# Wide moving operand for the gate and up units of the second block

## The reference

```python
def swiglu_2(x, w_gate, w_up, w_down):
    return (jax.nn.silu(x @ w_gate) * (x @ w_up)) @ w_down

def rmsnorm_2(x, g):
    x32 = x.astype(jnp.float32)
    y = x32 * lax.rsqrt(jnp.mean(x32 * x32, axis=-1, keepdims=True) + EPS)
    return (y * g.astype(jnp.float32)).astype(x.dtype)

# hybrid_layer, called for two layers
x = x + 0.5 * swiglu_2(rmsnorm_2(x, ffn1_norm), ffn1_gate, ffn1_up, ffn1_down)
...                                    # the mixers
x = x + 0.5 * swiglu_2(rmsnorm_2(x, ffn2_norm), ffn2_gate, ffn2_up, ffn2_down)
```

## Time and profile before

| | us |
|---|---|
| median of three runs | 2867.47 |
| span of the profiled execution | 2866.6 |
| TensorE busy | 2796.4 (98%) |
| VectorE busy | 1820.9 (64%) |
| ScalarE busy | 1341.1 (47%) |
| GpSimd busy | 789.2 (28%) |

### The profile page before, as it was taken

How to read it: one execution, slowest core, us unless ns; L and a number is a source line. 1 busy time by engine, 2 the same in 40 slices (tenths; PEclk the granted TensorE clock), 3 DMA queues, 4 the chain that set the end, 5 groups by cost and what they waited for, 6 DMA issues and landing times.

```text
span 2866.6 us, 59491 instructions
## 1 busy us (share of the span) xinstructions
PE 2796.4 (98%) x23696; PEld 2684.6 (94%) x23696; DVE 1820.9 (64%) x2505; ACT 1341.1 (47%) x1872; POOL 789.2 (28%) x768
## 2 busy tenths in 40 slices
PE   6999999999999999999999999999999999999999
PEld 4999999999999999999987898999889999997999
DVE  4655746687647557566466765665876566488664
ACT  3434434444435444344345444445764444377443
POOL 1322411123304214133001330320743223146330
PEclk9999999999999999999999999999999999999999
DMA  8765666575666756766631454555325555541554
GB/s 304 256 243 205 231 232 209 193 248 193 235 233 204 243 202 209 240 201 230 239 104 60 147 183 154 176 193 184 131 82 186 195 174 184 192 156 60 178 183 152
DMA packets 151712, 546.44 MB, mean 191 GB/s; under 512 B 16688, under 2 KB 20576, under 8 KB 151136
## 3 DMA queue, kind: packets, MB, share of 16 engines
q1 hardware_dynamic: 147632, 534.84, 54.9%
q10 hardware_dynamic: 3888, 8.86, 0.9%
HBM read 541.80 MB, written 1.84 MB: 190 GB/s over the span
## 4 chain that ended last, share of the span: by engine, by line
PE 91%; DVE 5%; ACT 1%; issue 1%; ACTq 1%; DMA 0%; SPq 0%; DVEq 0%
PE ps L410 28%; PE ps L412 28%; PE ps L411 28%; PE ps L437 2%; DVE w_lo L390 1%; PE ps L821 1%; PE ps L805 1%; PE ps L794 1%; ACTq L1558 0%; DVE xT L1952 0%; DVE h_lo L1602 0%; DVE xT L1968 0%; PE ps L889 0%; PE ps L696 0%; DVE m L1967 0%
## 5 line engine op out<-in xcount | busy, mean ns | idle before, releaser
L390 DVE TENSOR_TENSOR w_lo<-raw,w_hi 128x1024 fp32r<-128x1024 f32 x874 | 1135.4, 1315 | 634.5 <-ACT w_hi L382 632.1
L410 PE MATMUL ps<-h_hi,w_hi 128*128 128x256 f32 (+1 forms) x4928 | 1405.8, 285 | 24.3 <-DVE h_lo L1602 12.2
L412 PE MATMUL ps<-h_hi,w_lo 128*128 128x256 f32 (+1 forms) x4928 | 1393.8, 283 | 0.0
L411 PE MATMUL ps<-h_lo,w_hi 128*128 128x256 f32 (+1 forms) x4928 | 1388.5, 282 | 0.0
L382 ACT ACTIVATE w_hi<-raw 128x1024 fp32r<-128x1024 f32 x874 | 894.4, 1053 | 515.5 <-PE ps L412 514.5
L410 PEld LDWEIGHTS ps<-h_hi,w_hi 128*128 128x128 f32 x4928 | 929.9, 189 | 45.2 <-issue 25.2
L412 PEld LDWEIGHTS ps<-h_hi,w_lo 128*128 128x128 f32 x4928 | 947.9, 192 | 0.0
L411 PEld LDWEIGHTS ps<-h_lo,w_hi 128*128 128x128 f32 x4928 | 932.2, 189 | 0.8
L2266 POOL CAST u_hi<-ut 128x256 fp32r<-128x256 f32 (+1 forms) x258 | 234.3, 908 | 1370.4 <-DVE ut L1760 787.1
L410 PE MATMUL ps<-u_hi,w_hi 128*128 128x256 f32 (+1 forms) x2064 | 588.4, 285 | 0.2 <-DVE ut L1654 0.2
L411 PE MATMUL ps<-u_lo,w_hi 128*128 128x256 f32 (+1 forms) x2064 | 581.2, 282 | 0.0
(11 more groups left out here) (317 smaller groups left out, 1761.7 us busy)
## 6 DMA issues: line engine op xcount, KB each, us to landing
raw<-wst SPq DMA_DIRECT2D x874, 512.0 KB, 3.4
modraw<-wmod SPq DMA_DIRECT2D x132, 512.0 KB, 5.3
headraw<-wmod SPq DMA_DIRECT2D x12, 512.0 KB, 10.0
mtab<-mixtabs ACTq DMA_DIRECT2D x2, 1673.5 KB, 7.1
xT<-xin ACTq DMA_DIRECT2D x2, 1024.0 KB, 23.6
atab<-attabs ACTq DMA_DIRECT2D x1, 1024.0 KB, 6.2
out<-xT SPq DMA_DIRECT2D x1, 1024.0 KB, 4.8
skew<-sqb ACTq DMA_DIRECT2D x1, 768.0 KB, 3.3
```

Source lines behind the costliest of these rows:

```text
L390: dve.tensor_tensor(w_lo[:, s, :], raw[:, s, :], w_hi[:, s, :], ALU.subtract).then_inc(S("lo_ready"), 1)
L410: pe.matmul(psum, wh, hi, start=start, stop=False)
L411: pe.matmul(psum, wh, lo, start=False, stop=False)
L412: return pe.matmul(psum, wl, hi, start=False, stop=stop)
```

## The change

In the four unshifted `gu` stages a tile becomes two matmuls in place of three. `h_hi` and `h_lo` become the two halves of one tensor `h2`. The high weights are multiplied with both halves at once, 512 columns into a whole PSUM bank (columns 0 to 255 the high half, 256 to 511 the low half), and the low weights with the high half alone, added to columns 0 to 255. The two halves of a bank then have to be summed: ScalarE copies the low halves of the gate bank and the up bank of a pair to `sq` in one instruction of 512 columns (`low_halves`), VectorE adds the high halves to them into `gt` (`add_halves`), GpSimd multiplies both by `rstd` (`scale_pair`), ScalarE applies Silu (`gate`), and VectorE makes the product (`product`). Each unit now has a bank of its own: 4 and 5 for the first pair, then 0 to 3. The shifted `gu` stage, the stages `out` and the whole first block stay as they are.

```diff
+        def tile_wide(pe, s, k, bank, both, start, stop):
+            wh, wl = w_hi[:, s, P * k:P * (k + 1)], w_lo[:, s, P * k:P * (k + 1)]
+            pe.matmul(ps[:, bank, :].rearrange("p (a t) -> p a t", a=2), wh, both, start=start, stop=False)
+            return pe.matmul(ps[:, bank, 0:T], wl, both[:, 0, :], start=False, stop=stop)
...
+            def low_halves(c, i, j, banks):
+                n = FC * c["wide"] + 2 * i + j
+                act.wait_ge(S("unit_done"), c["unit"] + 2 * j + 2 + 4 * i)
+                if not (isinstance(n, int) and n < 2):
+                    act.wait_ge(S("halves_added"), n - 1)
+                act.activation(sq[:, j, :].rearrange("p (a t) -> p a t", a=2), ps[:, banks, T:2 * T],
+                               ACT.Copy).then_inc(S("low_copied"), 1)
+
+            def wide_gu_act(c):
+                b = c["unit"]
+                low_halves(c, 0, 0, slice(4, 6))
+                gate(c, 0, 0)
+                split_hi(act, b + 5)
+                low_halves(c, 0, 1, slice(2, 4))
+                with act.Fori(1, FC // 2) as i:
+                    split_hi(act, b + 2, i)
+                    gate(c, i - 1, 1)
+                    split_hi(act, b + 3, i)
+                    low_halves(c, i, 0, slice(0, 2))
+                    split_hi(act, b + 4, i)
+                    gate(c, i, 0)
+                    split_hi(act, b + 5, i)
+                    low_halves(c, i, 1, slice(2, 4))
+                gate(c, FC // 2 - 1, 1)
...
+            def add_halves(c, i, j, banks):
+                n = FC * c["wide"] + 2 * i + j
+                both = gt[:, j, :].rearrange("p (a t) -> p a t", a=2)
+                dve.wait_ge(S("low_copied"), n + 1)
+                dve.tensor_tensor(both, ps[:, banks, 0:T], sq[:, j, :].rearrange("p (a t) -> p a t", a=2),
+                                  ALU.add).then_inc(S("halves_added"), 1)
+            def product(c, i, j):
+                dve.wait_ge(S("silu_done"), FC * c["ffn"] + 2 * i + (j + 1))
+                dve.wait_ge(S("ulo_ready"), c["hid"] + 2 * i + (j + 1))
+                dve.tensor_tensor(ut[:, j, 0:T], gt[:, j, 0:T], gt[:, j, T:2 * T], ALU.mult).then_inc(S("gated"), 1)
...
+            def scale_pair(c, i, j):
+                both = gt[:, j, :].rearrange("p (a t) -> p a t", a=2)
+                pool.wait_ge(S("halves_added"), FC * c["wide"] + 2 * i + j + 1)
+                pool.tensor_tensor(both, both, rstd[:, 0:T].unsqueeze(1).broadcast_to([P, 2, T]),
+                                   ALU.mult).then_inc(S("gate_scaled"), 1)
```

More of the change, by code:

```diff
@@ L141, in make_plan @@
     c = dict(unit=REACHED["dense"], norm=0, pre2=0, x=0, out=0, post=0, ffn=REACHED["ffn"], fin=0,
-             hid=REACHED["hid"], h=0, early_n=0)
+             hid=REACHED["hid"], h=0, early_n=0, wide=0)
     def add(kind, **k):
@@ L158, in gu @@
         c["fin"] += 1
+        c["wide"] += not shift
         c["hid"] += FC
@@ L242, in build @@
             z_lo = sb("z_lo", [P, DC, 2 * T], F32, c1)
-        h_hi = sb("h_hi", [P, DC, 2 * T], F32R)
-        h_lo = sb("h_lo", [P, DC, 2 * T], F32R)
+        h2 = sb("h2", [P, 2, DC, 2 * T], F32R)
+        h_hi, h_lo = h2[:, 0], h2[:, 1]
         w_hi = sb("w_hi", [P, RING, D], F32R)
@@ L501, in in_first, with wide_unit @@
             mm.then_inc(S(done), 1)
+        def wide_unit(pe, d, i, bank):
+            s = d % RING
+            pe.wait_ge(S("lo_ready"), d + 4 * i + 1)
+            for k in range(DC):
+                mm = tile_wide(pe, s, k, bank, h2[:, :, k, 0:T], k == 0, k == DC - 1)
+            mm.then_inc(S("unit_done"), 1)
         def in_unit(pe, d, i, bank, N, step=4, h=None, hi=h_hi, lo=h_lo):
@@ L714, in first_units @@
                     for n in range(2):
-                        mm = tile(pe, (b + n) % RING, k, ps[:, 4 + n, 0:N], h_hi[:, k, 0:N], h_lo[:, k, 0:N], k == 0, k == DC - 1)
+                        if c["shift"]:
+                            mm = tile(pe, (b + n) % RING, k, ps[:, 4 + n, 0:N], h_hi[:, k, 0:N], h_lo[:, k, 0:N], k == 0, k == DC - 1)
+                        else:
+                            mm = tile_wide(pe, (b + n) % RING, k, 4 + n, h2[:, :, k, 0:T], k == 0, k == DC - 1)
                         if k == DC - 1:
@@ L722, in gu_pe @@
                 first_units(c, before[1])
+                if not c["shift"]:
+                    wide_unit(pe, b + 2, 0, 2)
+                    wide_unit(pe, b + 3, 0, 3)
+                    with pe.Fori(1, FC // 2) as i:
+                        for j in range(2):
+                            wide_unit(pe, b + 2 * j, i, 2 * j)
+                            wide_unit(pe, b + 2 * j + 1, i, 2 * j + 1)
+                    return
                 in_unit(pe, b + 2, 0, 1, N)
@@ L1314, in first_qkv_act @@
                 hi_upto(act, d + 14)
+            def low_halves(c, i, j, banks):
[21 more added lines that the diff above has]
+                gate(c, FC // 2 - 1, 1)
             def gu_act(c):
                 b = c["unit"]
+                if not c["shift"]:
+                    return wide_gu_act(c)
                 for j in range(2):
@@ L1618, in pre2_dve, with wide_gu_dve @@
                 recip(c, T)
+            def add_halves(c, i, j, banks):
[8 more added lines that the diff above has]
+                dve.tensor_tensor(ut[:, j, 0:T], gt[:, j, 0:T], gt[:, j, T:2 * T], ALU.mult).then_inc(S("gated"), 1)
+            def wide_gu_dve(c):
+                d = c["unit"]
+                add_halves(c, 0, 0, slice(4, 6))
+                product(c, 0, 0)
+                split_lo(dve, d + 5)
+                add_halves(c, 0, 1, slice(2, 4))
+                with dve.Fori(1, FC // 2) as i:
+                    split_lo(dve, d + 2, i)
+                    product(c, i - 1, 1)
+                    split_lo(dve, d + 3, i)
+                    add_halves(c, i, 0, slice(0, 2))
+                    split_lo(dve, d + 4, i)
+                    product(c, i, 0)
+                    split_lo(dve, d + 5, i)
+                    add_halves(c, i, 1, slice(2, 4))
+                product(c, FC // 2 - 1, 1)
             def gu_dve(c):
                 d = c["unit"]
+                if not c["shift"]:
+                    return wide_gu_dve(c)
                 for j in range(2):
@@ L2283, in position_pool, with wide_gu_pool @@
                         chain_pool(c["chain"], step)
+            def scale_pair(c, i, j):
[3 more added lines that the diff above has]
+                                   ALU.mult).then_inc(S("gate_scaled"), 1)
+            def wide_gu_pool(c):
+                scale_pair(c, 0, 0)
+                scale_pair(c, 0, 1)
+                split_hidden(c, 0, 0, T, u_hi, u_lo)
+                with pool.Fori(1, FC // 2) as i:
+                    scale_pair(c, i, 0)
+                    split_hidden(c, 2 * i - 1, 1, T, u_hi, u_lo)
+                    scale_pair(c, i, 1)
+                    split_hidden(c, 2 * i, 0, T, u_hi, u_lo)
+                split_hidden(c, FC - 1, 1, T, u_hi, u_lo)
             for c in FIRST:
@@ L2295, in _ @@
                     pre2_pool(c)
+                elif kind == "gu" and not c["shift"]:
+                    wide_gu_pool(c)
                 elif kind == "gu":
```

## The result

The changed kernel takes 2881.93 us (median of 4 runs, 2880.60 to 2885.69) against 2867.93 us before (4 runs, 2866.15 to 2868.39): a ratio of 1.0046, 95% interval 1.0033 to 1.0058, so 14 us slower. The forecast was 2885. The profiled execution has a span of 2883.2 us (before 2866.6) and a mean granted clock of 0.992 (before 0.995). It is the slowest of the four runs, 3.8 us above their median; the other three have spans of 2878.8 to 2880.7 us at a mean clock of 0.994.

A forecast was written before the change was run, and what follows sets the result against it. TensorE was taken to bound the kernel before, a loop over the other engines the changed one. Span 2866.6 + 9.8 (stages) + 8.0 (clock) = 2884.4, plus 0.9 to the median: 2885 us, range 2858 to 2902.

The forecast's parts named there:

- C against S0: In each pair's loop, GpSimd's multiply waits for VectorE's low split, ending 2.38 us after that split's start.
- C: GpSimd's multiplication of a pair's gate and up by `rstd`; forecast 1.29 us with no split beside it.
- S0: VectorE's low split for the first unit of the pair two later; forecast to start 0.61 us after the add's start.
- The loop of 5.56 us: Changed stages: engine orders close a loop without TensorE, 5.56 us a pair, longer than TensorE's forecast 5.34.
- TensorE's tile: Changed stages: a tile falls from 353 ns to 331 to 334, as 512 columns (213 ns) plus 256 (118 ns).
- TensorE waits 0.2 us a pair: Changed stages: TensorE waits some 0.2 us for the low split at the start of each pair's second unit.
- the second rival: Wide matmul gains nothing, pair stays 5.65 us, only stage ends cost (2.5 + 0.8 us a stage): 2880 us; chance 0.07.
- The stage's end: In `out`, the chain from the last low split to TensorE's resumption takes 4.24 us; TensorE idles some 4.4 us.
- S1: VectorE's low split for the second unit of the pair two later; forecast 1.07 us after its high split starts.
- M: VectorE's product of a pair, after the Silu; 0.43 us in the forecast chain at the stage's end.
- A: VectorE's add of the high halves to the copied low halves of a pair; forecast 0.69 us.
- The clock: Half clock behind TensorE's idle time in `out` costs 2.0 us a stage, 8 in all, bounds 0 and 10.

The follow-up runs named there:

- experiment 2: Changed kernel with VectorE's product moved ahead of both low splits of a pair; 2898.73 us, ratio 1.0104 to the kernel before.
- experiment 7: Changed kernel with GpSimd's multiply cut into two of 256 elements, gate's half first, Silu waiting for that half alone; 2874.13 us, ratio 1.0015.
- experiment 8: Changed kernel with GpSimd's multiply cut into two of 256 elements, up's half first, so Silu waits for both; 2904.26 us, ratio 1.0117.
- experiment 1: Changed kernel with TensorE's fifth tile in `out` waiting for the last add in place of the last product; 2867.58 us, ratio 0.9996.
- experiment 3: Changed kernel with the multiplication by `rstd` moved from GpSimd to VectorE, right behind the add; 2866.65 us, ratio 0.9991.
- experiment 4: Changed kernel with VectorE multiplying by `rstd` and `out` waiting for the last add; 2860.25 us, ratio 0.9967.

## Why the prediction was right, and where it was not

**C against S0: right.** C starts behind S0, is held, and ends 2.37 us behind its start (forecast 2.38). Experiments 2, 7 and 8 fix the rule from three sides: with no split beside it C lasts 1.29; a first half alone ends 1.82 behind S0's start; as two instructions it ends 2.55 behind it. The Trainium skill (SBUF — State Buffer, Who interferes with whom) says that two such instructions exclude each other and that the one issued first keeps the port. The rows of experiment 7 agree and show both orders within two pairs (1.74 for a half behind the split; 0.73 ahead of it, and the split at 1.72).

**The loop of 5.56 us: right.** It measures 5.55 to 5.56 in stages one, three and four. Each of its links measured what was forecast, give or take 0.03. With C's end moved 0.55 earlier (experiment 7) the pairs went to TensorE's pace, and with it 0.18 later (experiment 8) to 5.70.

**TensorE's tile: mis-sized.** The step "a stream of 512 columns (213 ns, which hides a weight load ...)" failed. The wide matmul takes 229 ns, not 213, so a tile gains 6.6 ns and not 19 to 22. What stands on top of the columns grows with their number (11, 14, 16 ns at 256, 384, 512), so it is not a weight load that a long stream hides; that rows 3 show nothing on top was read at half clock, and did not carry over. What it is stays open.

**TensorE waits 0.2 us a pair: wrong, by that term.** A pair takes TensorE 5.55 us, and the loop 5.56. TensorE and the loop run side by side, and what is left over at the stage's end is the lateness of the first round plus the long chain. That fits a gap of 3.9 us where 4.4 was forecast. It also puts the outcome close to the second rival (2880, no gain from the wide matmul), which had the mechanism on TensorE nearly right. The time alone, 2881.93 against 2885 and 2880, can't tell the two apart; the gaps of 3.9 us (2.5 by that rival) and the experiments do. With the loop out of the way (experiment 7) the time is 2874, and with the loop 0.15 us longer it is 2904.

**The stage's end: right.** The chain from the last S1 through M to TensorE's resumption came out in the order listed, at 4.11 us in stage one (1915.54 to 1919.65) where 4.24 was forecast, and experiment 1 gives 14 us back by cutting it at A.

**The clock: right, for the profiled execution.** 7.4 us against 8.0. The three faster runs had a higher clock, and no traces of them tell where. With gaps of up to 1.7 us (experiments 1 and 3) nothing is lost.

**The sum: right for the reasons given, with one pair of errors that offset each other.** TensorE's slower tile means a smaller gap at the end, and it means no waits inside the stage; the length of the stage is that of the loop either way. The forecast of 2885 is what the profiled execution took (2885.69); the median is 3 us below it.

Left open: in stage two of the profiled changed kernel TensorE's tile goes from 346.7 to 353.3 ns at 2163.2 us and stays there, with nothing in the other engines' rows to account for it.
```profile
2179.84 0.40 PE L418 MATMUL ps<-h,w_hi 128*128 128x512 f32 x1
2180.07 0.28 PE L419 MATMUL ps<-h,w_lo 128*128 128x256 f32 x1
2180.19 0.40 PE L418 MATMUL ps<-h,w_hi 128*128 128x512 f32 x1
```
There the loop catches up, the stage goes as the second rival has it, and the gap is 2.58. None of the 16 stages of experiments 1, 3, 4 and 7 did the same, so the cause was not found.

## What to carry to other kernels

When work is moved from the engine that looks full to one that looks idle, write down the loop that the orders of the engines close, with the place where the two engines can't run together, and compare its sum with the pace of the bound engine. The end of a stage is priced apart: count the chain from the last matmul to the first use of its banks, and let a bank go at the last instruction that reads it, not at the last that uses its value. Here this one line was worth 14 us, as much as the whole change had cost.

## What the runs showed that was not expected

- A matmul of this type at full clock stands 117.5 ns before the next at 256 columns, 174 at 384 and 229 at 512: 11, 14 and 16 ns over the bare columns. At half clock it was 213 for 256 with nothing on top.
- Gaps of the same length do not cost the same clock. In experiment 2 all four gaps are 2.30 us: behind that of stage one the granted clock is 1.00 (window 1922.50 to 1925.00), behind that of stage two 0.54 (2275.50 to 2278.00); in experiment 7 gaps of 2.18 us were followed by these:
```profile
2267.30:2270.00 2.70, 2.68 (x14) 2.68 (x15) 2.61 (x2) 1.08 (x3) 2.62 (x3) 0.59 0.03 12
2457.30:2460.00 2.70, 2.70 (x22) 2.70 (x23) 2.62 (x2) 1.97 (x3) 2.62 (x3) 1.00 0.02 8
```
- VectorE's product of 256 elements is held by GpSimd's split too: 0.96 us in place of 0.42 (experiment 2: 0.97).
